# Squares by channel tiles and 32 by 32 turns in place of TensorE transposes at the end of block one

## The reference

```
# end of block one
x  = x + memory_cross_attention(hx, hm, xa_wq, xa_wkv, xa_wo)   # this is x2
x3 = rms_norm(x, final_norm_g)                                   # block one's result
# start of block two
h    = rms_norm_2(x3, g_pre)
proj = h @ w_in_2            # its GV columns are the first that are computed
...
x = x3 + rms_norm_2(merged @ w_out_2, g_post)
```

## Time and profile before

| what | value |
|---|---|
| median of 3 runs (lowest, highest) | 3279.27 us (3279.14, 3280.43) |
| profiled execution, its own time | 3279.35 us |
| its span from first to last instruction | 3277.6 us |
| PE busy | 3260.3 us (99%) |
| POOL, ACT, DVE busy | 1382.9, 1085.2, 779.9 us (42%, 33%, 24%) |
| 64 transposes of x2 by PE | between 1027 and 1068 us |
| stage xwo, tiles 2 to 15 | 1018.7 to 1063.0 us |
| stage gv, up to the next stage | 1063.0 to 1152.7 us |

### The profile page before, as it was taken

One profiled execution on the slowest core, in us unless ns is written; L12 is line 12 of the kernel. 1 busy time (PEld: TensorE's weight loads), 2 busy tenths in 40 slices (PEclk: granted clock), 3 DMA queues, 4 the chain that ended last, 5 costly groups with the idle time before them and its releaser, 6 DMA issues.

```text
span 3277.6 us, 39124 instructions
## 1 busy us (share of the span) xinstructions
PE 3260.3 (99%) x14911; PEld 2692.1 (82%) x14911; DVE 779.9 (24%) x1251; ACT 1085.2 (33%) x1668; POOL 1382.9 (42%) x593
## 2 busy tenths in 40 slices
PE   9999999999999999999999999999999999999999
PEld 8877788888888878888888888888888888888887
DVE  3574321013124444300111101111111134300201
ACT  6542323233246444322223323333222222222332
POOL 7633333434443433444443343434444434444443
PEclk9999999999999999999999999999999999999999
DMA  7522323333442422333332333233333333333342
GB/s 284 175 77 71 84 65 85 88 83 106 115 125 90 126 73 78 89 101 98 87 99 81 90 90 90 78 89 96 97 96 96 96 97 91 102 97 98 104 158 97
DMA packets 536619, 331.02 MB, mean 101 GB/s; under 512 B 17196, under 2 KB 511412, under 8 KB 535220
## 3 DMA queue, kind: packets, MB, share of 16 engines
q1 hardware_dynamic: 522228, 304.82, 32.8%
q10 hardware_dynamic: 14272, 24.52, 2.2%
HBM read 316.71 MB, written 12.58 MB: 100 GB/s over the span
## 4 chain that ended last, share of the span: by engine, by line
PE 97%; DVE 1%; ACT 1%; issue 0%; DMA 0%; ACTq 0%; POOL 0%; DVEq 0%; POOLq 0%
PE proj L701 78%; PE s L1492 3%; PE s L1186 1%; PE proj L1492 1%; PE t L1492 1%; PE t L726 1%; PE t L781 1%; PE proj L774 1%; PE s L781 1%; PE s L774 1%; PE t L1186 1%; PE proj L1186 1%; PE t L701 1%; PE s L1011 1%; PE s L726 1%; PE s L992 1%
## 5 line engine op out<-in xcount | busy, mean ns | idle before, releaser
L680 POOL TENSOR_TENSOR w_lo<-raw,w_hi 128x1024 fp32r<-128x1024 f32 x564 | 1380.7, 2459 | 1868.8 <-ACT w_hi L1531 1842.4
L701 PE MATMUL proj<-ht_hi,w_hi 128*128 128x512 f32 x3408 | 1350.0, 396 | 3.4 <-DVEq L3078 3.4
L701 PE MATMUL proj<-ht_hi,w_lo 128*128 128x512 f32 x3408 | 1328.3, 390 | 0.0
L701 PE MATMUL proj<-ht_lo,w_hi 128*128 128x512 f32 x3408 | 1327.1, 389 | 0.0
L1531 ACT ACTIVATE w_hi<-raw 128x1024 fp32r<-128x1024 f32 x528 | 543.5, 1054 | 865.0 <-PE proj L701 701.7
L701 PEld LDWEIGHTS proj<-ht_hi,w_hi 128*128 128x128 f32 x3408 | 640.5, 188 | 139.4 <-issue 6.6
L701 PEld LDWEIGHTS proj<-ht_hi,w_lo 128*128 128x128 f32 x3408 | 640.0, 188 | 135.2
L701 PEld LDWEIGHTS proj<-ht_lo,w_hi 128*128 128x128 f32 x3408 | 640.6, 188 | 134.1 <-issue 4.8
L701 PE MATMUL proj<-yh,w_hi 128*128 128x512 f32 x368 | 143.2, 389 | 0.0
L701 PE MATMUL proj<-yl,w_hi 128*128 128x512 f32 x368 | 143.2, 389 | 0.0
L701 PE MATMUL proj<-yh,w_lo 128*128 128x512 f32 x368 | 143.2, 389 | 0.0
(11 more groups left out here) (587 smaller groups left out, 2996.1 us busy)
## 6 DMA issues: line engine op xcount, KB each, us to landing
raw<-in_w_in_dram SPq DMA_DIRECT2D x404, 512.0 KB, 3.8
raw<-in_w_out_dram SPq DMA_DIRECT2D x64, 512.0 KB, 3.9
raw<-in_xa_wkv_dram SPq DMA_DIRECT2D x16, 512.0 KB, 6.8
raw<-in_w_mem_kv_dram SPq DMA_DIRECT2D x16, 512.0 KB, 3.4
raw<-in_w_br_gla_dram SPq DMA_DIRECT2D x16, 512.0 KB, 3.9
raw<-in_w_br_pool_dram SPq DMA_DIRECT2D x16, 512.0 KB, 3.8
mem_tok<-in_mem_dram SPq DMA_DIRECT2D x8, 512.0 KB, 7.9
x_tok<-in_x_dram ACTq DMA_DIRECT2D x4, 1024.0 KB, 8.1
```

Of the source, the lines that this page charges most:

```text
L680: pool.tensor_tensor(w_lo[:, slot, :], raw[:, slot, :], w_hi[:, slot, :].bitcast(F32), ALU.subtract).then_inc(lo_done, 1)
L701: ins = pe.matmul(dst, w, x[:, kt, c0:c1], start=first and n == 0 and m == 0, stop=last and n == len(kts) - 1 and m == 2)
```

## The change

PE no longer transposes x2. Instead:

- For every channel tile n ACT makes two squares, of x2 and of x2 times final_norm_g (`x2_squares`), into the tile `x2_q`, and DVE adds this pair of 512 columns to `x2_acc` (`x2_add`, one addition of 128x1024). Tile 0 writes to `x2_acc` directly.
- PE sums `x2_acc` over partitions with eight small matmuls (4 columns of ones) ahead of `v_rows(1, 0, ...)`, and now waits there for `x2_added`; DVE reads the sums from PSUM.
- In the loop over k of stage gv, DVE multiplies tile k of x2 by final_norm_g into `x3u` and turns it in blocks of 32 by 32 into `x3v`. ACT stores it with four DMAs for each k, each of 32 partitions: 32 x 16 runs of 32 floats (128 bytes), which puts each block in its place of `x3_spill`. DVE waits for the stores of tile k - 2 ahead of the turn of tile k.
- The load of `gf_row` is gone.

```diff
-            def x2_rows(g):
-                pe.wait_ge(bank_free[0], Q2["xwo"] + 2 * g + 2)
-                pe.wait_ge(bank_free[1], Q2["xwo"] + 2 * g + 2)
-                for t in range(NT):
-                    if g:
-                        pe.wait_ge(x3_kept, 4 * g - 3 + t)
-                    transposes(S[t], [xy[:, 4 * g + n, t * P:(t + 1) * P] for n in range(4)]).then_inc(x2_t, 1)
...
-                if n in (4, 8, 12):
-                    x2_rows(n // 4 - 1)
...
-            x2_rows(3)
             for kt in range(1, 4):
                 for t in range(NT):
                     v_rows(0, t, [kt])
-            pe.wait_ge(x3_kept, 13)
+            pe.wait_ge(x2_added, KT)
+            for x in range(2):
+                for t in range(NT):
+                    ins = pe.matmul(S[3][:, 16 * x + 4 * t:16 * x + 4 * t + 4], x2_acc[:, x, t * P:(t + 1) * P], ones[:, 0:4],
+                                    start=True, stop=True)
+            ins.then_inc(x2_sums, 1)
             v_rows(1, 0, range(4))
-            pe.wait_ge(x3_kept, 16)
             pe.wait_ge(h2_diag, NT)
...
# ACT, stage xwo
+            def x2_squares(n):
+
+                need(act, x2_added, n - 1)
+                dst = x2_q[n % 2] if n else x2_acc
+                act.activation(dst[:, 0, :], xy[:, n, :], ACT.Square).then_inc(x2_sq, 1)
+                act.activation(dst[:, 1, :], xy[:, n, :], ACT.Square, scale=col("final_norm_g", n)).then_inc(x2_sq, 1)
...
                     act.activation(ht_hi[:, n, :], xy[:, n, :], ACT.Copy, scale=col("g_pre", n)).then_inc(norm_hi, 1)
-            for t in range(NT):
-                x2_square(3, t)
-            for t in range(NT):
-                x3_square(3, t)
-            x3_store(3)
+                    x2_squares(n)
...
# ACT, loop over k of stage gv
+                act.wait_ge(x3_kept, k + 1)
+                for r in range(0, P, 32):
+                    act.dma_start(x3_spill[:, k * P + r:k * P + r + 32].rearrange("(b i) j -> i b j", i=32),
+                                  x3v[k % 2][r:r + 32, :].rearrange("p (b j) -> p b j", j=32)).then_inc(x3_out[k % 2], 16)
...
# DVE, stage xwo
+            def x2_add(n):
+
+                dve.wait_ge(x2_sq, 2 * n + 2)
+                dve.wait_ge(x2_added, n)
+                dve.tensor_tensor(x2_acc[:], x2_acc[:], x2_q[n % 2][:], ADD).then_inc(x2_added, 1)
...
+                if n == 2:
+                    dve.wait_ge(x2_sq, 2)
+                    dve.sem_inc(x2_added, 1)
+                elif n > 2:
+                    x2_add(n - 2)
             u_low(KT - 1)
+            x2_add(KT - 2)
+            x2_add(KT - 1)
+            dve.wait_ge(x2_sums, 1)
...
# DVE, loop over k of stage gv
+                dve.tensor_scalar(x3u[k % 2][:], xy[:, k, :], col("final_norm_g", k), None, MUL).then_inc(x3_scale, 1)
+                dve.wait_ge(x3_scale, k + 1)
+                if k > 1:
+                    dve.wait_ge(x3_out[k % 2], 64 * (k // 2))
+                dve.transpose(x3v[k % 2][:], x3u[k % 2][:]).then_inc(x3_kept, 1)
```

More of the change, by code:

```diff
@@ L282, in build @@
         o_hi, o_lo = behind_x3("o_hi", [P, 4, T], F32R), behind_x3("o_lo", [P, 4, T], F32R)
-        n_ss = behind_x3("n_ss", [P, 48])
-        gf_row = at("gf_row", [P, D], m_at)
+        x2_acc = at("x2_acc", [P, 2, T], m_at)
         lr_at = m_at + 7 * 2048
         lr_raw, lr_w = at("lr_raw", [P, KT, 16], lr_at), at("lr_w", [P, KT * 32 + 96], lr_at + 1024, F32R)
-        x3u = at("x3u", [P, NT, T], lr_at + 4096 + 64)
+        x2_q = [at(f"x2_q{i}", [P, 2, T], lr_at + 4096 + 64 + 4096 * i) for i in range(2)]
+        x3u = [at(f"x3u{i}", [P, T], lr_at + 4096 + 64 + 2048 * i) for i in range(2)]
+        x3v = [at(f"x3v{i}", [P, T], lr_at + 8192 + 64 + 2048 * i) for i in range(2)]
         n_diag = at("n_diag", [P, NT, P], o_at)
@@ L401, in build @@
         gv_done, gv_act, gv_dve = sem("gv_done"), sem("gv_act"), sem("gv_dve")
-        gf_in, x2_t, x2_sq, x2_sq3 = [sem(n) for n in "gf_in x2_t x2_sq x2_sq3".split()]
-        x3_kept, x3_out, x2_ms, x2_root = [sem(n) for n in "x3_kept x3_out x2_ms x2_root".split()]
+        x2_sq, x2_added, x2_sums = [sem(n) for n in "x2_sq x2_added x2_sums".split()]
+        x3_scale, x3_kept, x2_ms, x2_root = [sem(n) for n in "x3_scale x3_kept x2_ms x2_root".split()]
+        x3_out = [sem("x3_out0"), sem("x3_out1")]
         h2_diag, r_pe, r_kept = [sem(n) for n in "h2_diag r_pe r_kept".split()]
@@ L1966, in _ @@
                            bias=eps_rms).then_inc(norm_root, 1)
-            act.dma_start(gf_row[:], a["final_norm_g"].rearrange("(o d) -> o d", o=1).to_broadcast([P, D])).then_inc(gf_in, 16)
             xa_query(1)
@@ L2021, in _ @@
                     ahead(H4["gv"], 1, 1)
[L2022 to L2030, removed]
                 if n < KT:
@@ L2072, in _ @@
                 act.activation(ht_hi[:, k, :], nt["t"][k % 2][:], ACT.Copy).then_inc(norm_hi, 1)
+                act.wait_ge(x3_kept, k + 1)
+                for r in range(0, P, 32):
+                    act.dma_start(x3_spill[:, k * P + r:k * P + r + 32].rearrange("(b i) j -> i b j", i=32),
+                                  x3v[k % 2][r:r + 32, :].rearrange("p (b j) -> p b j", j=32)).then_inc(x3_out[k % 2], 16)
             wh_high(0)
             v_kept(1)
-            act.wait_ge(x3_out, 64)
+            for out in x3_out:
+                act.wait_ge(out, 32 * KT)
             def merge(name, branch, parts=("first", "rest")):
@@ L2944, in _ @@
             for n in range(KT):
[L2945 to L2948, removed]
                 if n % 2:
@@ L2955, in _ @@
                     u_low(n - 1)
-            for t in range(NT):
-                x3_rows(3, t)
+                if n == 2:
[3 more added lines that the diff above has]
+                    x2_add(n - 2)
             u_low(KT - 1)
-            dve.wait_ge(x2_sq3, 16)
+            x2_add(KT - 2)
+            x2_add(KT - 1)
+            dve.wait_ge(x2_sums, 1)
             ms = small[:, 40:48]
-            link(dve.tensor_reduce(ms, n_ss[:, 0:32].rearrange("p (t g) -> p t g", g=4), AX, ADD))
-            link(dve.tensor_scalar(ms, ms, 1.0 / D, None, MUL))
+            link(dve.tensor_scalar(ms, S[3][:, 0:32].rearrange("p (t c) -> p t c", c=4)[:, :, 0], 1.0 / D, None, MUL))
             link(dve.tensor_scalar(r_x3, r_x3, RMS_EPS, None, ADD))
```

19 lines of the change are left out of this document (removed).

## The result

| | before | after |
|---|---|---|
| median (lowest, highest), 20 runs each | 3279.15 us (3276.89, 3280.49) | 3283.97 us (3280.85, 3285.01) |
| profiled execution, its own time | 3279.35 us | 3282.61 us |
| its span | 3277.6 us | 3280.8 us |

The ratio is 1.0014, with a 95% interval of 1.0008 to 1.0020: slower by 0.14%, some 4.8 us, which is less than the 0.2% that I had set as "no change", but more than nothing.

A forecast was written before the change was run, and what follows sets the result against it. PE was taken to bound the kernel, with DVE becoming the pace in xwo: -7.0 + 1.7 - 0.3 + 4.2 + 5.0 = +3.6, less 0.3, so 3279.35 + 3.3 = 3282.6 us; own range 3280 to 3285.5, whole range 3273.5 to 3288.

The forecast's parts named there:

- PE's own balance: PE alone: -7.0 us for the transposes, +1.7 for the new small matmuls, so -5.3; -0.3 for old waits.
- the second rival: DVE keeps up in xwo, so PE does not stall: -5.6 us, 3273.8; chance 0.2.
- The pace of DVE: In xwo, w_lo locks out DVE's SBUF operations; a pair of tiles costs DVE 6.6 us against PE's 5.5.
- the waits on xy: PE stalls on DVE's xy additions through xwo and into gv: 4.2 us, the first near tile 10.
- The weights of gv: At gv's entry w_lo comes late: stalls of 1.0, 0.3 and 3.7 us ahead of kt 1, 2 and 3.
- rival 3: PE's clock falls to 1.2 GHz behind the 3.7 us stall before kt 3: +1.6 us, 3284.3; chance 0.2.
- The old waits: Waits of PE already in xwo before the change, about 0.3 us, go away.
- the same bookkeeping: The stall sum applied to the kernel before was said to end 0.3 us late, so +3.6 became +3.3.
- The sums: Eight new matmuls with 4 columns on PE in gv: +1.7 us.
- The root of the squares: In gv it must come under 12 matmuls of 2.7 us; wait of 0 to 0.6 us, taken as 0.
- the loop over k: In gv, product, turn and DMA issues fit under PE's 5.44 us a tile (DVE 5.1): costed at nothing.
- Slow stores: In gv's loop, 128-byte store packets stall PE from 27 ns each; at 40 ns +12 us, about 3295; chance 0.13.

The follow-up runs named there:

- experiment 1: The changed kernel without the x2_add additions, so the sums are those of tile 0 alone: 3273.62 us, ratio 0.9983.
- experiment 8: The changed kernel, sums still in SBUF, with the addition ahead of ht_lo in odd tiles of xwo: 3279.12 us, ratio 0.9999.
- experiment 3: The changed kernel with x2_acc in two PSUM banks, each addition two of 512 columns with one PSUM operand: 3279.51 us, ratio 1.0002.
- experiment 2: The changed kernel without the turn, the product stored with one DMA for each k in rows of 2 KB: 3284.05 us, ratio 1.0014.
- experiment 6: The changed kernel with x2_acc in PSUM and, in odd tiles of xwo, the additions ahead of ht_lo: 3273.41 us, ratio 0.9982.

## Why the prediction was right, and where it was off

**The direction and the place: right.** PE's own balance was put at -5.3 and -0.3 (3273.8 in all, the second rival's number); experiment 1 measured -5.7 in the stretch and 3273.62 us. All of the loss lies in xwo and at the entry into gv.

**The pace of DVE: right, with a smaller bill.** `x2_add` was put at 1.21 and 1.13 a piece; it takes 1.21 to 1.22, the next start 1.13 later. The pair was put at 6.6 and is 6.42. The 0.2 make the first full wait come at tile 12 and not near tile 10, and the waits on xy 3.3 us in place of 4.2. In the part of it that I stressed, that an addition of two SBUF tiles of 1024 columns is locked out as well, the rows say yes: 2.82 beside w_lo in experiment 8, 3.39 at 1063.73 in the changed kernel. The rule of the Trainium skill ("SBUF — State Buffer", Who interferes with whom) holds there. But in xwo the lock fell on ht_lo, and experiment 3 showed that taking the addition out of it changes the pair by nothing.

**The weights of gv: right in the chain, somewhat too dear.** I put waits of 1.0, 0.3 and 3.7 us ahead of kt 1, 2 and 3. Measured: 0.72, none, and 1.87, with the 0.11 and the distances 3.1 us in all in place of 5.0. The chain came as described: the squares of tile 15 behind a locked addition (ACT idle 3.05 us on it), then w_hi, then the w_lo of 1069.43, which takes 3.03 us since the last additions run as it begins, and ends at 1072.46. That is 2.2 ahead of the 1074.7 that I put in the old trace's time. 0.84 of it is the start of this execution and 0.9 the pair that takes 6.42 and not 6.6, five times. The rest is POOL's turn: I let it wait for DVE ahead of the w_lo of kt 1, which began at once, and from the end of this one to the start of kt 2's I put 0.7, where 0.31 passed. But the 1.87 is so short only because PE had lost 1.6 us to the clock on the way; where it had not, in the profile of experiment 2, the wait is 3.40 and the term 4.7 of the 5.0.

**The clock: what the sum left out.** The forecast took the clock as full and left its fall to rival 3, with a chance of 0.2 and 1.6 us behind kt 3. It fell there in both profiles of this stretch, for 1.3 us in one and 2.4 in the other; the fall behind kt 1 in the first of them was free. With the free stretch counted as the wait that it replaced, the forecast's 9.2 us of waits were 8.0, and 1.3 of clock came on top: two errors that cancel. That the profiled time, 3282.61, is the forecast's to the digit is luck, and owes something to the 0.84 by which this execution was ahead, too. The median, 3283.97, lies closer to rival 3's 3284.3. The clock of the executions without a profile isn't shown.

**Two small terms.** The old waits were put at 0.3 and are 0.5. And I took 0.3 off the sum because the same bookkeeping was to end 0.3 late for the kernel before; it doesn't. From 1062.6, with 1.75 and 60 matmuls at 0.227, it comes to 1078.0, 0.4 ahead of 1078.36. Without this step the forecast would have been +3.6, 3283.0.

**The sums: 2.1 in place of 1.7.** They stand behind a stretch at the lower clock; in experiment 6, at full clock, they take 1067.76 to 1069.46 = 1.70.

**The root of the squares and the loop over k at nothing: right.** The spreading of the root follows the last of its 12 matmuls at 1081.52 without idle time. ACT's table load, which I had dropping out, is still there, but at 1069.37, long ahead of the root. In the loop the product takes 0.48, 2.63 where it falls behind w_lo, the turn 0.71 and the four issues about 2.1 us of ACT's queue a tile (0.524 each). DVE is busy for 51.14 of 65 us there, 4.3 a tile, between the 2.7 that I put for its own work and the 5.1 with a whole w_lo to wait for, and PE waits for nothing.

**Slow stores: didn't happen.** 13 ns a packet, a landing of 2.3 us, and experiment 2 shows that longer rows would bring nothing.

## What to carry to other kernels

An operation added to an engine that is busy for a quarter of the time can make that engine the pace of a stage: what counts is the load within the period of the stage, with the time for which a neighbour locks it out. In this kernel (3284.0 to 3273.4 us) it paid to sort DVE's work: where it is of both kinds, lay the operations that have an operand in PSUM beside GpSimd's, and the ones that read and write SBUF alone behind it; in stage xwo neither the operand nor the order helped by itself. And where PE waits at a seam, two cures for the same seam don't add up: look for the stage that fills the lag before mending the seam. A slow stretch ahead of a longer wait for another engine costs nothing, so what the clock costs can't be read from slow matmuls alone.

## What the runs showed of the hardware that I had not expected

- An operation with a single tile input can be locked out as well, which I had not reckoned with: the product `x3u` of 128x512 takes 0.48, and 2.63 at 1124.71, 0.07 behind the start of a w_lo that took 2.42. The xy addition of the same size, which reads PSUM, keeps its 0.68 beside w_lo, and additions with a PSUM operand and a PSUM result 1.28 for two.
- It works both ways: w_lo takes 2.41 alone, and 3.02 in experiment 8, where the addition of 1.21 was running when it began.
- A DMA of 512 runs of 128 bytes costs ACT 0.5 us to issue, and the DMA engines 13 ns a run.
- The lower clock can follow idle times of 0.97 and 0.72 us on PE in one execution, stay away behind the same two in another (experiment 2), and fail to follow one of 2.52.
